# Stages that end with three weight units taken a row tile at a time, in place of four

## The reference, cut to what matters

```
for l in range(2):                                    # B0, B1
    h = rms_norm_2(x, mix_pre_norm[l])
    ... y = gt0 * (o_dn @ w_branch_dn) + gt1 * (o_pool @ w_branch_pool) + gt2 * (o_ret @ w_branch_ret)
    x = x + rms_norm_2(y @ w_out[l], mix_post_norm[l])            # 1024 -> 1024
    h = rms_norm_2(x, ffn_pre_norm[l])
    x = x + rms_norm_2((silu(h @ w_gate) * (h @ w_up)) @ w_down, ffn_post_norm[l])   # 1024 -> 2816 -> 1024
```

## Time and profile before

| | |
|---|---|
| median of 3 runs | 1435.18 us (1434.91 to 1435.49) |
| profiled execution | 1437.14 us, its span 1435.2 us |
| PE busy | 1401.2 us (98%), x7603 |
| PE weight loads | 1203.5 us (84%) |
| DVE busy | 990.1 us (69%) |
| ACT busy | 753.7 us (53%) |
| POOL busy | 60.9 us (4%) |
| mean DMA rate | 157 GB/s |
| mean granted TensorE clock | 0.996 of full speed |

### The profile page before, as it was taken

One profiled execution on the slowest core, in us unless ns is written; L12 is line 12 of the kernel. 1 busy time (PEld: TensorE's weight loads), 2 busy tenths in 40 slices (PEclk: granted clock), 3 DMA queues, 4 the chain that ended last, 5 costly groups with the idle time before them and its releaser, 6 DMA issues.

```text
span 1435.2 us, 18932 instructions
## 1 busy us (share of the span) xinstructions
PE 1401.2 (98%) x7603; PEld 1203.5 (84%) x7603; DVE 990.1 (69%) x1199; ACT 753.7 (53%) x1061; POOL 60.9 (4%) x46
## 2 busy tenths in 40 slices
PE   7999999999999999999999999989999999999998
PEld 6988888988887988898877888879888888788886
DVE  6689777698765679647776564457795568756553
ACT  6764766764764575434454443355643444544432
POOL 2002000002000000000000000000100000000000
PEclk9999999999999999999999999999999999999999
DMA  8544235544234654334445565464533244366553
GB/s 287 190 157 147 91 137 183 177 140 144 100 126 152 215 176 147 118 96 154 142 152 176 178 194 170 163 225 138 169 134 118 90 134 173 118 213 195 178 175 118
DMA packets 139125, 225.72 MB, mean 157 GB/s; under 512 B 8032, under 2 KB 54432, under 8 KB 138912
## 3 DMA queue, kind: packets, MB, share of 16 engines
q1 hardware_dynamic: 137376, 221.90, 47.1%
q10 hardware_dynamic: 1664, 2.63, 0.5%
HBM read 223.46 MB, written 1.05 MB: 156 GB/s over the span
## 4 chain that ended last, share of the span: by engine, by line
PE 87%; DVE 6%; ACT 4%; issue 1%; DMA 1%; POOL 1%; SPq 0%; ACTq 0%; DVEq 0%
PE gp L576 63%; PE gp L565 8%; PE mp L841 5%; PE mp L548 4%; PE mp L683 2%; DVE wt_rest L1415 2%; DVE arena L1409 1%; PE mp L737 1%; DVE arena L1877 1%; POOL rs_out L2119 1%; DMA wt<-in_w_in 1%; PE mp L804 1%; PE mp L834 0%; PE mp L711 0%; PE mp L697 0%
## 5 line engine op out<-in xcount | busy, mean ns | idle before, releaser
L1415 DVE TENSOR_TENSOR wt_rest<-wt,wt_hi 128x1024 fp32r<-128x1024 f32 x156 | 184.1, 1221 | 78.4 <-ACT wt_hi L1027 77.7
L1027 ACT ACTIVATE wt_hi<-wt 128x1024 fp32r<-128x1024 f32 x156 | 156.6, 1055 | 106.8 <-DMA wt<-in_ffn_up 52.6
L1415 DVE TENSOR_TENSOR wt_rest<-wt,mix_hi 128x1024 fp32r<-128x1024 f32 x136 | 160.8, 1221 | 64.4 <-ACT mix_hi L1027 63.5
L1027 ACT ACTIVATE mix_hi<-wt 128x1024 fp32r<-128x1024 f32 x136 | 139.9, 1062 | 108.2 <-PE gp L576 57.0
L576 PE MATMUL gp<-wt_rest,mix_hT_hi 128*128 128x512 f32 x384 | 149.7, 390 | 0.0
L576 PE MATMUL gp<-wt_hi,hT_hi 128*128 128x512 f32 x352 | 140.3, 399 | 4.8 <-DVE wt_rest L1415 4.0
L576 PE MATMUL gp<-mix_hi,mix_hT_hi 128*128 128x512 f32 x352 | 140.6, 399 | 4.2 <-DVE wt_rest L1415 3.1
L576 PE MATMUL gp<-wt_hi,hT_rest 128*128 128x512 f32 x352 | 137.5, 391 | 0.0
L576 PE MATMUL gp<-mix_hi,mix_hT_rest 128*128 128x512 f32 x352 | 137.3, 390 | 0.0
L576 PE MATMUL gp<-wt_rest,hT_hi 128*128 128x512 f32 x352 | 137.1, 390 | 0.0
L1027 ACT ACTIVATE first_hi<-wt 128x1024 fp32r<-128x1024 f32 x104 | 106.4, 1061 | 48.6 <-PE gp L576 38.1
(11 more groups left out here) (318 smaller groups left out, 3056.5 us busy)
## 6 DMA issues: line engine op xcount, KB each, us to landing
wt<-in_w_in SPq DMA_DIRECT2D x100, 1024.0 KB, 5.0
wt<-in_ffn_gate SPq DMA_DIRECT2D x44, 512.0 KB, 4.1
wt<-in_ffn_up SPq DMA_DIRECT2D x44, 512.0 KB, 5.1
wt<-in_w_out SPq DMA_DIRECT2D x20, 1024.0 KB, 5.0
wt<-in_ffn_down SPq DMA_DIRECT2D x20, 1024.0 KB, 5.0
wt<-in_w_mem_kv SPq DMA_DIRECT2D x8, 1024.0 KB, 6.3
wt<-in_w_branch_pool SPq DMA_DIRECT2D x4, 1024.0 KB, 5.1
wt<-in_w_branch_ret SPq DMA_DIRECT2D x4, 1024.0 KB, 5.1
```

The source lines that it names most:

```text
L1027: nc.scalar.activation(rounded_part(u)[:, k:k + nk, :], wt[:, u % SLOTS, k:k + nk, :], ACT.Copy)\
L1415: return nc.vector.tensor_tensor(o, i0, i1, ALU.subtract)
```

## The change

The mixer's end multiplies M0a for both tiles first; the tail is M1a, M0b, M1b. The transposes of the second half of the sum and the wait for them are at the same places between the units, so that M0a of tile 1 now stands ahead of them. The transposes of the new rows stand ahead of M1b of the second pass, where they stood between the parts of M0b. In the feed-forward's end E1 has three units multiplied for both tiles and three in the tail, and the transposes stand ahead of the last (two-k) unit of the second pass; they stood between the parts of the one before it. Nothing on the other engines is changed, and no instruction is added or removed.

```diff
                 split_units(s("BD1"), 1, halfway=lambda: sum_transposes(0))
                 sums_taken(0)
-                split_tail(SLOTS, {(0, 1): lambda: sum_transposes(1), (0, 2): lambda: sums_taken(1),
-                                   (1, 2, "halfway"): lambda: tile_transposes(s("fT"), DEPTH + 2 * l + 1, 0)})
+                split_units(s("M0"), 1)
+                split_tail(SLOTS - 1, {(0, 0): lambda: sum_transposes(1), (0, 1): lambda: sums_taken(1),
+                                       (1, 2): lambda: tile_transposes(s("fT"), DEPTH + 2 * l + 1, 0)})
                 rows_first(s("fT"), DEPTH + 2 * l + 1)
...
-                split_units(s("E1"), -(-KF // UNIT_K) - SLOTS)
-                split_tail(SLOTS, {(1, 2, "halfway"): lambda: tile_transposes(f"B{l + 1}.xT", DEPTH + 2 * l + 2, 0)} if l + 1 < DEPTH else {})
+                split_units(s("E1"), -(-KF // UNIT_K) - SLOTS + 1)
+                split_tail(SLOTS - 1, {(1, 2): lambda: tile_transposes(f"B{l + 1}.xT", DEPTH + 2 * l + 2, 0)} if l + 1 < DEPTH else {})
```

## The result

| | before | changed |
|---|---|---|
| median, first comparison (5 runs each) | 1435.33 us | 1440.82 us |
| ratio, 95% interval | | 1.0037 [1.0023, 1.0051] |
| median, second comparison (16 and 7 runs) | 1435.79 us | 1440.49 us |
| ratio, 95% interval | | 1.0029 [1.0017, 1.0040] |
| profiled execution, its span | 1437.14, 1435.2 us | 1440.88, 1438.8 us |

The change makes the kernel slower by 5.3 us in the one comparison and 4.2 us in the other (ratio less one, times the median before; the plain differences of the medians are 5.5 and 4.7). Both intervals lie above 1. The forecast was +4.5 us, 1439.7.

A forecast was written before the change was run, and what follows sets the result against it. PE holds 87% of the chain and loses time only at borders, waiting for DVE behind tile 0's transposes. 2 x 1.3 + 1.9 + 0 = +4.5 us on 1435.18 gives 1439.7 us, range 1437.0 to 1441.9.

The forecast's parts named there:

- The norm chain: At the borders: normed rows need 6.06 us after the first pass, so transposes start at 6.16 instead of 6.82 us.
- The mixer's ends: Mixer ends of B0 and B1: PE's take-over moves by +1.3 us each, bounds 0.6 and 2.1.
- The gain ahead of M0b: Mixer ends: 0.75 us won of PE's idle of about 1.3 us, as M0a of tile 1 stands ahead.
- The feed-forward's end: Feed-forward's end of B0: transposes move +2.07 us and PE's take-over +1.9 us, bounds 1.2 and 2.2.
- the credit for the load: Feed-forward's end: 0.15 us credited because ACT no longer waits 2.85 us for RKa's load.
- The last tail: Last tail, without transposes: DVE is free in time, so 0 us, bounds 0 and +0.3.
- No slack behind the transposes: Mixer borders: DVE's work from F0a on stands back to back, so PE's take-over moves with the transposes, +1.3 us.
- loads don't enter: Mixer ends: each load is issued no later than before, so loads add nothing to the +1.3 us.
- The clock: Ahead of RQa and at B1's small matmuls: taken as 0; rival of a fall, about +2.1 us, 1441.8 us, 8%.
- Faster: Rival: PE at the borders really waits for loads, which slots freed earlier remove; -2.9 us, 1432.3 us, 5%.
- The norm chain isn't hit: Rival: the norm ends within 5.46 us of the pass, transposes start on PE's arrival; +2.4 us, 1437.6 us, 12%.
- Mixer gain absent: Rival: M0b still starts a full unit late at the mixer ends; +6.0 us in all, 1441.2 us, 10%.

The follow-up runs named there:

- four_late: Kernel before, four units in the tail, with tile 0's transposes 36 matmuls after the first pass in place of 30: 1439.78 us, ratio 1.0027 to the kernel before.
- four_early: Kernel before, four units in the tail, with tile 0's transposes 24 matmuls after the first pass in place of 30: 1434.04 us, ratio 0.9985 to the kernel before.
- e_only: Kernel before with only the feed-forward's end changed, in both layers: 1437.77 us, ratio 1.0011 to the kernel before.
- no_norm: Changed kernel, but PE transposes the identity matrix in place of tile 0's normed rows at the three borders: 1437.40 us, ratio 1.0012 to the kernel before.
- rest_first_four: Kernel before, PE order kept, with the next stage's first unit rounded and its rests taken earlier on ACT and DVE: 1455.43 us, ratio 1.0134.
- three_early: Changed kernel with the transposes one part earlier, 18 matmuls after the first pass in place of 24: 1440.75 us, ratio 1.0030 to the kernel before.

## Why the prediction was right

The forecast 1439.7 us was 1.1 us under the first median; the schedule part is confirmed term by term, and the rest is within what the two comparisons differ. That the median comes so close is in part luck: the first interval reaches from +3.3 to +7.3 us, and the clock, which I put at 0, moves single executions by over 1 us.

- **The norm chain.** From ACT's square at 736.19 to the norm's end at 741.29 + 0.76 (0.77 in the chain) it is 5.86 us, against the 5.85 read before. The hand-over is 742.19 less 742.05, so 0.14 us where I put 0.1. PE waits 0.6 us ahead of both kinds of transposes, 0.7 expected. Right.
- **The mixer's ends.** Sized +1.3 each, measured +1.21 and +1.19. M0b started 0.2 us sooner than I had worked out: 730.45 - 0.74 (what came before) = 729.71, not 729.9. The gain ahead of M0b, 0.75 in the forecast, was thus 0.94. F0a came late by 747.73 - 745.78 - 0.74 = 1.21 us, as much as the border, so DVE and ACT behind the transposes had nothing to give.
- **The feed-forward's end.** Sized +1.9, measured +2.03. The transposes moved by 936.25 - 932.20 - 1.95 = 2.10 (2.07 expected, the 1.95 being what came before) and the credit for the load was 0.07 rather than 0.15. RKa's wait went, as expected, and was worth next to nothing. (RQa's slot came free two and a half tile units earlier, not three, as the last unit is half as long; the sum doesn't use that.)
- **The last tail.** 0 expected, -0.1 measured.
- **No slack behind the transposes.** Assumed from rows that stand back to back; four_late shows it one to one at the mixers, and four_early from the other side in B0, at the mixer and the feed-forward. At the mixer of B1 four_early ran into a load; "loads don't enter" was right for the change, not for every order.
- **The clock.** The mis-sized term. I gave its fall ahead of RQa 8% and a price of 1.4 to 2.8 us. It fell in three of five profiled executions with such an idle, and cost 0.7 us. The 2.8 us of a fall were right, but I took off only the idle rows behind RQa, 1.17 + 0.27 = 1.44 us. An idle is counted from the end of a matmul's row, and such a row (0.39 us) is longer than the distance to the next (0.2275), so every pause is longer than its idle: over the 36 matmuls the pauses were 10.37 - 8.19 = 2.18 us before and 2.07 in the changed kernel. It didn't fall in the two profiled executions of the changed kernel; how often it does in its timed runs isn't shown. The other term that I put at 0, the small matmuls of B1, gave back 1.2 us between the two profiled executions; which of the two the timed runs are like isn't shown. The Trainium skill ("TensorE: Matmul & The Clock Gate", section "The HAM clock gate") speaks of the lower clock after an idle window, and of a window that runs free of the kernel. The falls of e_only, no_norm and four_late agree with the first; that the same idle came with a fall in e_only and without one in the changed kernel fits the second, but no run here shows such a window.
- **The rivals.** "Faster" fell with e_only and with the load that ACT no longer waits for. "The norm chain isn't hit" fell with the 0.6 us waits. "Mixer gain absent" fell with M0b's wait, 0.74 to 0.29 us (about 0.5 expected).

## What to carry to other kernels

When a stage's last units are split by row tile so that the first tile's epilogue can run under the second pass, one unit fewer starts the epilogue up to a unit later (1.8 us later at the mixers and 2.7 at the feed-forward here), and what is queued behind the dependent work moves with it, less what that work stood too late before (0.66 us here). Put the dependent work of the first tile where its data gets ready (here 6.2 us, 27 matmuls, behind the first pass), not later: PE's idle there was free, because PE waited for the same queue afterwards anyway. Look at the loads again after such a move; four_early's gain at one of three borders went to a load. A slot that is freed earlier is worth nothing by itself while the work on the load stands in a queue behind the late work; moved ahead of it, it turned a loss of 4 to 5 us into a gain of nearly 4. When you weigh a slower PE against its pauses, take the pauses from the starts of the matmuls, not from the idle in the rows.

## What the runs showed of the hardware

TensorE's granted clock fell in or just behind the idle of 3.07 to 3.08 us ahead of RQa in three of five profiled executions and held in two. In rest_first_four PE idled 5.92 us ahead of the transposes at that end, and the clock fell too (0.50 from 942 to 948 us). An idle of 1.74 us ahead of RQa in the kernel before left it alone. In three_early PE idled 1.96 us ahead of the transposes of B0's mixer end, 1.94 at the feed-forward's end and 1.96 at B1's mixer end, in one execution: the clock held at the first (1.00 over 740.00 to 744.00), and after the other two it was mostly at the 1.2 GHz level (0.58 over 1238.00 to 1242.00 at B1's, and this row at the feed-forward's end):

```profile
934.00:938.00 4.00, 3.34 (x13) 2.99 (x14) 1.70 (x6) 2.40 (x9) 0.00 (x0) 0.61 0.48 185
```

So the length of a wait alone doesn't settle it here. The price was 0.7 us where PE had pauses behind it (e_only), a quarter of the 2.8 us that a fall cost where PE was the bound. Behind the small matmuls of 16 columns at the start of B1, 3.5 us of them at full clock, the clock fell in twelve of the thirteen profiled executions and held in rest_first_four, where they took 3.47 us.
